# A router that reads un-normalised tokens, and joint choice rounds, in a one-core encoder layer

## What is computed

```python
mix = jnp.concatenate([attn_out, conv_out], axis=-1) @ w_out
x = x + gate1 * mix
h2 = rms_norm(x, norm_ffn) * (1 + scale2) + shift2
# expert_choice_ffn, for each group by itself
aff = jax.nn.softmax((t @ w_router).astype(jnp.float32), axis=-1)
g, idx = lax.top_k(aff.T, cap)          # cap = 128 for the prompt, 32 for the sample
xe = t[idx]
hid = jax.nn.silu(jnp.einsum('ecd,edf->ecf', xe, w_gate)) * jnp.einsum('ecd,edf->ecf', xe, w_up)
ye = jnp.einsum('ecf,efd->ecd', hid, w_down) * g[..., None].astype(t.dtype)
```

## Time and profile before

| | |
|---|---|
| median of three runs | 1550.4 us (1549.52 to 1552.12) |
| the profiled execution | 1550.12 us, of which 1548.1 us are the span of the records |
| busy in the span | PE 1449.1 us (94%), DVE 1118.1 us (72%), ACT 799.0 us (52%), POOL 192.7 us (12%) |
| chain that ended last | PE 83%, DVE 6%, ACT 6%, DMA 2% |

### The profile page before, as it was taken

One profiled execution on the slowest core, in us unless ns is written; L12 is line 12 of the kernel. 1 busy time (PEld: TensorE's weight loads), 2 busy tenths in 40 slices (PEclk: granted clock), 3 DMA queues, 4 the chain that ended last, 5 costly groups with the idle time before them and its releaser, 6 DMA issues.

```text
span 1548.1 us, 27140 instructions
## 1 busy us (share of the span) xinstructions
PE 1449.1 (94%) x10061; PEld 1078.7 (70%) x10061; DVE 1118.1 (72%) x1586; ACT 799.0 (52%) x1312; POOL 192.7 (12%) x210
## 2 busy tenths in 40 slices
PE   4999999889999989988399999999999999999996
PEld 1777787537878867765277777777777777777774
DVE  1258988898868876357677877778777787877774
ACT  2222232147777773232456666566665666655662
POOL 0022012200000001121101101211011211111110
PEclk9999999989999999998599999999999999999998
DMA  9400001453000002233878888988889898889951
GB/s 339 161 1 28 28 1 55 158 223 111 2 2 1 2 28 82 96 126 124 314 247 283 293 283 282 305 289 295 276 290 303 283 303 273 290 287 301 304 181 17
DMA packets 113682, 281.31 MB, mean 182 GB/s; under 512 B 10581, under 2 KB 16825, under 8 KB 110552
## 3 DMA queue, kind: packets, MB, share of 16 engines
q1 hardware_dynamic: 105944, 259.54, 47.5%
q0 software_dynamic: 7680, 20.98, 6.0%
HBM read 259.51 MB, written 20.97 MB: 181 GB/s over the span
## 4 chain that ended last, share of the span: by engine, by line
PE 83%; DVE 6%; ACT 6%; DMA 2%; issue 1%; POOL 1%; SPq 0%; ACTq 0%; DVEq 0%; POOLq 0%
PE banks L1434 11%; PE banks L1409 11%; PE banks L1414 10%; PE banks L1410 10%; PE banks L1094 8%; PE banks L1303 7%; PE banks L1105 6%; PE banks L1254 4%; PE banks L1231 4%; PE banks L1241 4%; ACT xs_t L973 2%; DVE c_t L1634 2%; DMA ada<-in_ada_w 2%; PE banks L1441 1%; PE banks L1467 1%
## 5 line engine op out<-in xcount | busy, mean ns | idle before, releaser
L1939 DVE TENSOR_TENSOR low<-raw,high 128x1024 fp32r<-128x1024 f32 x384 | 447.9, 1219 | 1.0
L952 ACT ACTIVATE high<-raw 128x1024 fp32r<-128x1024 f32 x384 | 380.5, 1052 | 0.8
L1634 DVE SCALAR_TENSOR_TENSOR c_t<-a_t,taps,c_t 128x256 f32<-128x256 f32 (+2 forms) x360 | 215.2, 663 | 0.5
L1409 PE MATMUL banks<-high,x_hi 128*128 128x512 f32 x512 | 208.5, 407 | 0.0
L1410 PE MATMUL banks<-high,x_lo 128*128 128x512 f32 x512 | 200.1, 391 | 0.0
L1414 PE MATMUL banks<-low,x_hi 128*128 128x512 f32 x512 | 158.6, 391 | 1.1 <-DVE low L1939 1.1
L1094 PE MATMUL banks<-h_t,w_u 128*128 128x256 f32 x640 | 144.0, 383 | 1.2 <-DVE h_t L1584 1.2
L1094 PEld LDWEIGHTS banks<-h_t,w_u 128*128 128x128 f32 x640 | 121.3, 192 | 17.2 <-issue 1.4
L1409 PEld LDWEIGHTS banks<-high,x_hi 128*128 128x128 f32 x512 | 96.1, 188 | 32.9 <-issue 13.6
L1434 PE MATMUL banks<-raw,xs_t 128*32 128x256 f32 x2048 | 118.7, 384 | 0.0
L1736 DVE TENSOR_REDUCE negmax<-banks 128x1 f32<-128x1024 f32 (+1 forms) x80 | 85.0, 1063 | 43.0 <-PE banks L1231 42.8
(11 more groups left out here) (223 smaller groups left out, 2198.5 us busy)
## 6 DMA issues: line engine op xcount, KB each, us to landing
raw<-in_w_gate SPq DMA_DIRECT2D x128, 512.0 KB, 4.6
raw<-in_w_up SPq DMA_DIRECT2D x128, 512.0 KB, 5.9
raw<-in_w_down SPq DMA_DIRECT2D x64, 1024.0 KB, 5.1
ada<-in_ada_w SPq DMA_DIRECT2D x24, 1024.0 KB, 8.3
w_u<-in_w_in SPq DMA_DIRECT2D x4, 1024.0 KB, 19.3
x_in<-in_x_prompt SPq DMA_DIRECT2D x4, 1024.0 KB, 5.0
w_out_sb<-in_w_out SPq DMA_DIRECT2D x1, 4096.0 KB, 13.7
x_again<-in_x_prompt SPq DMA_DIRECT2D x4, 1024.0 KB, 5.7
```

Source lines behind the costliest of these rows:

```text
L952: act.activation(high[c % RING][:, :], raw[ph][:, k, :], ACT.Copy).then_inc(hi_ready, 1)
L1409: pe.matmul(bank(b + h), s_hi_k, w_high[:, half], start=(k == 0), stop=False)
L1634: dve.scalar_tensor_tensor(out=c_t[s][:, c, :], in0=a_t[:, c, bass.ds(k + o, n)], scalar=taps[:, c, bass.ds(k, 1)], in1=c_t[s][:, c, :], o ...
L1939: dve.tensor_tensor(low[ph][:, k, :], raw[ph][:, k, :], high[c % RING][:, :].bitcast(F32), ALU.subtract).then_inc(lo_ready, 1)
```

## The change

It has four parts.

1. **The router.** The transposes read `x1` instead of `xn2`. The scale is multiplied into the router's weights once (`split_router` on DVE makes `router_p` for the prompt and scales `router` in place for the sample), the shift becomes a bias of 16 numbers for each group (`make_bias`, eight small matmuls on PE), and the reciprocal root of each token is multiplied onto the logits in `shift_logits`, which has two more operations for it. `h2_out` becomes a plain copy, one instruction for 512 columns where it was two of 256. The root of tiles 7, 8 and 9 is still made, but the tokens of these three tiles are scaled by ACT (`xn_out`) instead of DVE.
2. **The order on PE.** `turn_x1`, `route` and `turn_logits` of a pair stand between halves of the next pair, the last ones between pieces of a half. The whole of tile 8 now stands ahead of the transposes of the prompt's softmax.
3. **The choice.** The sample's affinities go to partitions 64 to 79 of `aff_p`, whose other half POOL fills with the lowest value. Rounds 12 to 15 run on 80 partitions and so choose for the sample as well; its own four rounds are gone. The sample's work stands at other rounds.
4. **The transfers.** The second token tile of the sample is stored behind the second half of the gate and up weights, and `load_down(0)` waits until both gathers of expert 0 have landed.

```diff
             def turn_x1(p):
-                pe.wait_ge(xn2_ready, 2 * p + 2)
+                pe.wait_ge(x1_ready, 2 * p + 2)
...
-                                                xn2[:, a, P * (2 * i + c):P * (2 * i + c + 1)], ident[:, :])
+                                                x1[:, a, P * (2 * i + c):P * (2 * i + c + 1)], ident[:, :])
...
+            def make_bias():
+                pe.wait_ge(router_split, 4)
+                for k in range(KC):
+                    last = pe.matmul(bank(7)[:, NE * NT:NE * (NT + 2)], ones[:, :], router_b[:, k, :, :].rearrange("p g e -> p (g e)"),
+                                     start=(k == 0), stop=(k == KC - 1))
+                last.then_inc(bias_made, 1)
...
-            project_out(2 * NPAIR - 2, 0)
+            project_out(2 * NPAIR - 2, 0, 0, 6)
             turn_x1(NPAIR - 2)
-            turn_logits(NPAIR - 3)
+            project_out(2 * NPAIR - 2, 0, 6, KC)
             route(NPAIR - 2)
+            project_out(2 * NPAIR - 2, 1, 0, 2)
             turn_logits(NPAIR - 2).then_inc(logits_turned, 1)
+            project_out(2 * NPAIR - 2, 1, 2, KC)
             pe.wait_ge(aff_ready, 1)
...
-            project_out(2 * NPAIR - 2, 1)
             project_out(2 * NPAIR - 1, 0)
             project_out(2 * NPAIR - 1, 1)
...
             turn_logits(NPAIR - 1).then_inc(logits_turned, 1)
+            pe.wait_ge(mix_gated, NT)
+            for j in range(4):
+                last = mod_row(bank(3)[STRIP * j:STRIP * (j + 1), 0:256], STRIP * (2 + j // 2) + 1, 4 + j, 256 * (j % 2), 256)
+            last.then_inc(gate2_made, 1)
             pe.wait_ge(aff_ready, 2)
...
+            def xn_out(q):
+                act.wait_ge(x1_recip, q + 1)
+                act.activation(xn2[:, q % 2, :], x1[:, q % 2, :], ACT.Copy, scale=rs_x[:, q:q + 1]).then_inc(xn2_late, 1)
...
             for r in range(CAP_P // 8):
-                if r == 3:
+                if r == JOINT_FROM:
+                    dve.wait_ge(padding_made, 2)
+                    dve.wait_ge(aff_copied, 2)
+                top_eight(r)
+                if r == 0:
                     gate_mix(2 * NPAIR - 2)
+                if r == 4:
+                    recip_x1(2 * NPAIR - 2)
                 if r == 5:
-                    norm_x1(2 * NPAIR - 2)
-                if r == 6:
                     gate_mix(2 * NPAIR - 1)
-                if r == 8:
-                    norm_x1(2 * NPAIR - 1)
...
-                    for i in range(CAP_S // 8):
-                        top_eight(aff_s, top_s, idx_s, i, CAP_S // 8, top_s_step)
...
-            load_gate_up(0, 1)
+            sp.wait_ge(gathered_s, 16)
+            sp.wait_ge(gathered_p, 16)
             load_down(0)
```

More of the change, by code:

```diff
@@ L544, in _ @@
                 sp.dma_start(x_again[:, :, :], x_rows(p)).then_inc(x_reloaded, 16)
+                dst_y = y_s[0] if group(p) else y_p[0, 2 * P * p:2 * P * (p + 1)]
+                dst_n = xn_s if group(p) else xn_p[2 * P * p:2 * P * (p + 1)]
                 if p == NPAIR - 1:
@@ L698, in square_x @@
                 act.wait_ge(x_squared, 2 * p + 2)
-                act.activation(rt_x[:, :], ss_x[:, :], ACT.Sqrt, scale=1.0 / D, bias=eps_col[:, :]).then_inc(x_root, 1)
+                act.activation(rt_x[:, 0:2], ss_x[:, 0:2], ACT.Sqrt, scale=1.0 / D, bias=eps_col[:, :]).then_inc(x_root, 1)
             def x_out(p, i):
@@ L908, in h2_out @@
                     act.wait_ge(t2_ready[n % 2], n // 2 + 1)
[L909 to L914, removed]
+                    act.activation(h2_t[:, 2 * i:2 * i + 2, :], bank(4 + n % 2).rearrange("p (c q) -> p c q", c=2),
+                                   ACT.Copy).then_inc(t2_free[n % 2], 1)
             def logits_out(p):
@@ L923, in _ @@
                 tile_high(2 * p + 3)
-                norm2(2 * p + 1)
-                h2_out(p)
                 if p < NPAIR - 2:
+                    norm2(2 * p + 1)
+                    h2_out(p)
                     tile_high(2 * p + 4)
+                else:
+                    h2_out(p)
+                    norm2(2 * p + 1)
                 logits_out(p)
@@ L935, in _ @@
             exp_logits(0, aff_h[:, :, 0:3:2, :])
+            xn_out(2 * NPAIR - 3)
             norm2(2 * NPAIR - 2)
-            norm2(2 * NPAIR - 1)
[L938 to L942, removed]
+            for h in range(2):
+                act.wait_ge(gate2_made, h + 1)
+                act.activation(gate2_p[:, 512 * h:512 * h + 512], bank(h), ACT.Copy).then_inc(gate2_ready, 1)
+            xn_out(2 * NPAIR - 2)
+            h2_out(NPAIR - 1)
+            norm2(2 * NPAIR - 1)
             logits_out(NPAIR - 1)
             exp_logits(1, aff_r[:, :, :])
+            xn_out(2 * NPAIR - 1)
+            act.wait_ge(gate2_made, 3)
+            act.activation(gate2_s[:, :], bank(3)[:, 0:D // 4], ACT.Copy).then_inc(gate2_ready, 1)
             def split_high(e, c):
@@ L1291, in _, with project_out @@
             pe.wait_ge(probs_ready, HEADS_ALL)
-            def project_out(q, half):
+            def project_out(q, half, k0=0, k1=KC):
                 if q >= 2:
@@ L1298, in project_out @@
                 pe.wait_ge(s_lo_ready, q + 1)
-                for k in range(KC):
+                for k in range(k0, k1):
                     high = s_hi[:, q % 2, k, :]
@@ L1324, in route @@
                     pe.wait_ge(logits_copied, p)
+                scaled_router = router if group(p) else router_p
                 for k in range(KC):
                     j = k % 4
-                    last = pe.matmul(bank(6)[STRIP * j:STRIP * (j + 1), 0:2 * P], router[:, k, :], h2_t[:, k, :],
+                    last = pe.matmul(bank(6)[STRIP * j:STRIP * (j + 1), 0:2 * P], scaled_router[:, k, :], h2_t[:, k, :],
                                      start=(k < 4), stop=(k >= KC - 4))
@@ L1364, in _ @@
             for i in range(HT):
[L1365 removed]
+                last = pe.transpose(bank(6)[0:FILLED, P * i:P * (i + 1)], aff_h[:, i, :, :].rearrange("p h e -> p (h e)"), ident[:, :])
             last.then_inc(aff_turned, 1)
[L1367 removed]
             project_out(2 * NPAIR - 1, 0)
@@ L1393, in _ @@
             for i in range(2):
-                last = pe.transpose(bank(1)[:, RANKED * i:RANKED * (i + 1)], top_p[:, i, :], ident[0:RANKED, 0:RANKED])
+                last = pe.transpose(bank(1)[:, RANKED * i:RANKED * (i + 1)], top_p[0:RANKED, i, :], ident[0:RANKED, 0:RANKED])
             last.then_inc(top_turned, 1)
@@ L1824, in h2_out @@
                     dve.wait_ge(t2_ready[n % 2], n // 2 + 1)
-                    for c in range(2):
-                        k = 2 * i + c
-                        last = dve.tensor_scalar(h2_t[:, k, :], bank(4 + n % 2)[:, 256 * c:256 * (c + 1)], a2[:, k, g:g + 1],
-                                                 mod[:, SHIFT2 + k, g:g + 1], ALU.mult, ALU.add)
-                    last.then_inc(t2_free[n % 2], 1)
+                    dve.tensor_copy(h2_t[:, 2 * i:2 * i + 2, :], bank(4 + n % 2).rearrange("p (c q) -> p c q", c=2)).then_inc(t2_free[n % 2], 1)
             scale_span(2)
```

193 lines of the change are left out of this document (116 added, 77 removed).

## The result

The changed kernel takes 1537.17 us (median of 5 runs, 1533.77 to 1541.4) against 1550.4 beside it: ratio 0.9917 (its time over that of before), 95% interval 0.9901 to 0.9934. Measured once more with the experiments it was 1538.69, ratio 0.9924 (0.991 to 0.9938). The profiled execution is 1536.95 us, span 1535.1, mean granted clock 0.976.

A forecast was written before the change was run, and what follows sets the result against it. The path through the prompt's softmax, DVE's choice and the gather was taken as the bound: 5.8 us gained at the first round, 12.4 through the rounds, 15.7 with the gather, giving 1534.5 us; range 1531.5 to 1539.5.

The forecast's parts named there:

- The first round: Way to the prompt's softmax: tile 7 done at 684.2, rounds starting at 700.0, a gain of 5.8 us.
- the softmax is just hidden: Ahead of its transposes: softmax ready at 698.3, PE arriving at 698.7; without cover, each us late costs one.
- my sign of being wrong: At the choice's start: a first round later than 702 would make the prediction wrong; it was expected near 700.
- The rounds: Choice on DVE: 47.1 us becomes 39.5 without a wait, 5.7 of it from the sample's own stretch.
- The new waits: DVE waiting for the sample in rounds 9 and 11: 1.0 us together, from 0 to 3.5 with low clock throughout.
- rival (a): Sample's gate rows hold the choice: PE's clock stays low, DVE waits 3.5 us, time 1537.0; 15 in 100.
- The gather: Prompt gather for expert 0: lands in 4.3 us instead of 8.15, at 748.8, with the weights drained by then.
- the 1.3 us that I had estimated: At the prompt gather: the cost of sharing 0.52 MB in halves with the weights, giving a time of 1537.0.
- Behind the gather: After the gather: down weights there by 760, later loads and uses in time, so no loss was put.
- Rival (d): Experts' loop gives the lead back, following the transfers and not PE: 1545 to 1550.4; 4 in 100.
- (c): Last token store, behind 4.2 MB of weights, delays POOL's gathers; decides if landing near 758: 1550.4 to 1555; 4 in 100.
- my sign for them: Down weights of expert 0: landed by 760, after starting at 748.8 and needing 11 us.

The follow-up runs named there:

- the control: The changed kernel itself, unedited, measured and profiled again with the experiments: 1538.69 us, ratio 0.9924 to the kernel before.
- e8: e7 with the bias moved from inside tile 2 to PE's wait for x1 of tile 7, three pieces of tile 8 following later: ratio 0.9896.
- e11: The changed kernel with the prompt's softmax transposes behind the sixth of eight pieces of tile 8's second half: ratio 0.9916.
- e6: The changed kernel with the joint rounds undone, the sample chosen from in four rounds of its own: ratio 0.9938.
- e3: The changed kernel with the sample's gate rows on PE moved behind its softmax transposes: ratio 0.9917, median 1538.71 us.
- e4: The changed kernel with 18 unused matmuls of 512 columns on PE in its idle time ahead of tile 9's transposes: ratio 0.9914, median 1538.40 us.
- e1: The kernel before with only the down weights of expert 0 put behind both gathers: ratio 0.9981, 1548.40 us against 1551.73.
- e2: The changed kernel with the down weights issued as before, without the wait for the gathers: ratio 0.9925.
- e10: e9 with the prompt's softmax transposes behind the third instead of the eighth piece of tile 8's second half: ratio 0.9886.
- e9: e8 with seven more unused multiplications on TensorE between the gate rows and the first expert: ratio 0.9892.
- e7: The changed kernel with e4's 18 multiplications, gate rows behind the sample's softmax transposes, and last token store ahead of the second 4.2 MB of weights: ratio 0.9902.

## Why the prediction held, and where it was off

The direction, the places and, inside the range, the size held: 13.2 us (11.6 at the control) were measured for 15.9 predicted. From the stage's start to the rows taken up some 12 us were gained: 3.7 at the first round, 4.7 in the rounds, 3.8 at the gather, less 0.3 lost behind the rounds. By steps, counted from the stage's start:

- **The first round**, predicted at 115.9 (700.0), came at 118.0: 3.7 us of gain, not 5.8. Tile 7 was done at 101.5, not 100.1: three groups of 2.32 to 2.38 instead of 2.2, the bias 1.70 instead of 1.4, and 5.68 to 5.71 us for a half behind a router product where it is else 5.47 to 5.5. From there to the transposes it took 15.3 instead of 14.5. That the softmax is just hidden was right (done 1.6 us ahead). The term that was too small is the sum of PE's work ahead of the softmax transposes; e8 and e11 show that this order is what counts. A start at 584.1 would have put this round at 702.1 (the control has 701.96): at the edge of my sign of being wrong, a first round later than 702.
- **The rounds** themselves: 42.4 us less waits of 2.7 are 39.6, predicted 39.5. Eighty partitions cost nothing: MAX8 takes 0.69 us on 48 and on 80. e6 puts the joining at 5.7 us of DVE, as predicted. The scaling of tokens that moved to ACT has no run of its own; that the rounds came out as summed is all that speaks for its price.
- **The new waits** were put at 1.0 us and were 2.7 (4.3 in the control). I took the clock to come back behind the idle stretch, as it had in the projection, and to stay; in the first profile it came back for 3 us and fell again with the gate rows, in the control it stayed low. A pair of gate rows takes 0.99 us, where 0.55 was seen before the change. This is rival (a), to which I gave 15 in 100, waits of 3.5 us and the time of 1537.0: e3 removes the wait by order, e4 by the clock. The Trainium skill, "TensorE: Matmul & The Clock Gate", section "Part 1: The HAM clock gate", which I had cited for it, has sustained activity lift the clock; this trace agrees with the low clock after an idle stretch, but not with the lift: the records have PE busy for 6.00 of 6.00 us, and it stayed at 0.50. The measurement decides.
- **The gather** landed in 4.31 us, predicted 4.3. In e1 the weights alone account for 3.9 us. So the 1.3 us that I had estimated from the rule of the Trainium skill ("DMA: Bandwidth & Descriptors", section "Queues, rings and completion order") are not what this trace shows; whether the rule fails here or my working from it is open. In the new order the waits are worth only 1.5 us (e2), because the queue had mostly drained anyway.
- **Behind the gather** nothing was given back: 783.5 us before, 783.8 and 783.4 after. Rival (d) fell, and (c) did not decide, but its margin was smaller than I had it: the last store landed at 741.8 us, where my terms give 736.7 (I wrote 738), and POOL came for its first gather at 744.7. e4 shows it as the next limit. The down weights were not in by 760, my sign for them: the windows from 751 to 760 hold 2.7 MB of their 4.2; the rest of the span shows no loss by it.

In all the rows are taken up at 168.5 where the prediction has 764.5 less 15.7 less 584.1, or 164.7: 2.1 us at the first round and 1.7 at the waits. The profiled execution, 2.6 us above its forecast of 1534.4, is nearer than that only because it started its stage 1.3 us early: luck. The control's median is 4.2 us above the forecast.

## What to carry to other kernels

Where an engine's order is fixed, a result is late by all that stands ahead of its reader in that order: e8 made the logits 1.8 us earlier for nothing, e11 moved four transposes past two pieces of a tile and gained 1.4. When work is put into the idle time of one engine, ask what runs at a lower clock for having idled, and put last what nobody waits for. A change that removes work in front of a wait gives back only what the wait leaves: nearly half of the joined rounds' gain was lost that way until the waits went too.

## What the hardware showed

In e10 the records have PE busy 8.00 of 8.00 us between 734 and 742, with gate rows and added matmuls, and the granted clock was 0.50 throughout. In e8 it rose at about 758, some 4 us into the strips, in e9 at about 752, under 1 us into them. No run separates what raised it.

The choice instructions cost the same on more partitions: MAX8 of 512 columns takes 0.69 us and FIND_INDEX8 0.68, on 48 partitions and on 80.

The time goes with the mean clock in the changed kernel: the shortest of five runs is at the highest (1533.77 us at 0.977), the longest at the lowest (1541.4 at 0.970). Why it varies is open: with the clock held up in the sample's stretch, five runs of e4 lay within 1.4 us (1537.46 to 1538.86), but six of e7, which has the same added matmuls, spread over 5.3 (1532.83 to 1538.14).
